# Down-projection with tokens stationary: a decoder layer's MLP on one Trainium2 core

## What is computed

```python
D_MODEL = 2048; D_FF = 8192; LN_EPS = 1e-5; ALPHA = 2 ** 0.25
def layer_norm(x, g, b):
    mu = mean(x); var = mean(square(x - mu))        # over the features
    return (x - mu) * rsqrt(var + LN_EPS) * g + b
# the second half of merge_and_mlp, for every one of the 544 tokens
x1 = layer_norm(ALPHA * x + mixed @ w_out, ln1_g, ln1_b)
u  = maximum(x1 @ w_up, 0)                          # 2048 -> 8192
y  = layer_norm(ALPHA * x1 + (u * u) @ w_down, ln2_g, ln2_b)   # 8192 -> 2048
```

## Time and profile before

| what | value |
|---|---|
| median of three runs | 2963.66 us |
| span of the profiled execution | 2953.3 us |
| PE, DVE, ACT, POOL busy | 95, 64, 29, 7% |
| DVE adds of the down-projection (L2129), 128x544 | 512 of 722 ns |
| DVE remainders of weights (L2116), 128x1024 | 1220 ns |
| ACT roundings of weights (L2041), 128x1024 | 1059 ns |
| a load of w_up or w_down (512 KB), issue to landing | 4.4 us |
| DVE shift of the norm (L2332), when POOL is idle | 0.17 us |

### The profile page before, as it was taken

The page is one execution under the profiler, slowest core; times in us unless marked ns, Lnnn a source line. Parts: engine busy times, 40 slices in busy tenths (PEclk is TensorE's granted clock), DMA queues, the critical chain, the costliest instruction groups (busy, mean ns, idle before and its releaser), DMA issues. The chain is left out here.

```text
span 2953.3 us, 58897 instructions
## 1 busy us (share of the span) xinstructions
PE 2803.1 (95%) x25775; PEld 2658.4 (90%) x25775; DVE 1887.3 (64%) x2204; ACT 842.9 (29%) x1226; POOL 207.3 (7%) x226
## 2 busy tenths in 40 slices
PE   7999999999999887899899999999999999999995
PEld 7998889888887665899789999999999999999994
DVE  3264555455553685536877777777777777777775
ACT  2221222122212355213533233232232322322321
POOL 2011101110110321001000000000000000000003
PEclk9999999999999899999999999999999999999997
DMA  9489999999999722445122232332323323323222
GB/s 343 154 314 402 410 374 412 411 400 394 413 396 340 246 79 82 104 132 138 51 79 86 86 114 71 103 106 67 115 84 88 109 72 107 101 71 115 79 94 89
DMA packets 340851, 548.62 MB, mean 186 GB/s; under 512 B 20940, under 2 KB 244781, under 8 KB 330019
## 3 DMA queue, kind: packets, MB, share of 16 engines
q1 hardware_dynamic: 263682, 334.37, 34.0%
q0 software_dynamic: 13872, 141.28, 11.8%
q10 hardware_dynamic: 63040, 69.21, 6.9%
HBM read 508.96 MB, written 35.84 MB: 184 GB/s over the span
## 5 line engine op out<-in xcount | busy, mean ns | idle before, releaser
L2129 DVE SCALAR_TENSOR_TENSOR base<-big_G,base 128x544 f32<-128x544 f32 x512 | 369.6, 722 | 244.3 <-PE big_G L1964 244.3
L449 PE MATMUL prj_G<-prj_xh,prj_wh 128*128 128x280 f32 x1696 | 504.0, 297 | 20.8 <-DVE prj_wl L692 13.9
L451 PE MATMUL prj_G<-prj_xh,prj_wl 128*128 128x280 f32 x1696 | 498.5, 294 | 0.0
L450 PE MATMUL prj_G<-prj_xl,prj_wh 128*128 128x280 f32 x1696 | 497.8, 294 | 0.0
L699 DVE STREAM_TRANSPOSE prj_kT<-base 128x4096 f32<-128x4096 f32 x64 | 284.5, 4445 | 258.3 <-PE prj_S L482 258.3
L2041 ACT ACTIVATE wh<-raw 128x1024 fp32r<-128x1024 f32 x227 | 239.4, 1059 | 652.8 <-PE big_G L1964 542.8
L1962 PE MATMUL big_G<-ff_uh,wh 128*128 128x272 f32 x1360 | 392.3, 288 | 3.6 <-DVE base L2129 3.5
L1963 PE MATMUL big_G<-ff_ul,wh 128*128 128x272 f32 x1360 | 393.5, 289 | 0.0
L1964 PE MATMUL big_G<-ff_uh,wl 128*128 128x272 f32 x1360 | 393.4, 289 | 0.0
L449 PEld LDWEIGHTS prj_G<-prj_xh,prj_wh 128*128 128x128 f32 x1696 | 322.9, 190 | 46.3 <-issue 34.5
L2116 DVE TENSOR_TENSOR wl<-raw,wh 128x1024 fp32r<-128x1024 f32 x227 | 277.0, 1220 | 86.3 <-ACT wh L2041 86.3
(11 more groups left out here) (418 smaller groups left out, 6097.2 us busy)
## 6 DMA issues: line engine op xcount, KB each, us to landing
prj_v_nat<-in_cache_v SPq DMA_DIRECT2D x242, 512.0 KB, 7.6
raw<-in_w_down SPq DMA_DIRECT2D x128, 512.0 KB, 4.4
raw<-in_w_up SPq DMA_DIRECT2D x120, 512.0 KB, 4.4
prj_raw<-in_w_in ACTq DMA_DIRECT2D x103, 512.0 KB, 17.6
raw<-in_w_out SPq DMA_DIRECT2D x16, 1024.0 KB, 7.1
prj_scratch<-prj_stage ACTq DMA_DIRECT2D x53, 280.0 KB, 9.3
out_xr<-x_scratch SPq DMA_DIRECT2D x16, 544.0 KB, 4.0
base<-in_cache_v SPq DMA_DIRECT2D x14, 512.0 KB, 7.2
```

The costliest lines, as they stand in the source:

```text
L449: mm(out, w_hi[:, k, m], xh[:, k0 + k, cols], start=(first and k == 0), stop=False)
L450: mm(out, w_hi[:, k, m], xl[:, k0 + k, cols], start=False, stop=False)
L451: last = mm(out, w_lo[:, k, m], xh[:, k0 + k, cols], start=False, stop=(end and k == nk - 1))
L2129: V.scalar_tensor_tensor(out, G[2 + t % 2][:, :, 0:HALF_M], 1.0 / ALPHA, out, ALU.mult, ALU.add).then_inc(y_done, 1)
```

## The change

The closing sums are held the other way round, with tokens on partitions: `acc` is 4 tiles of 128 prompt tokens by 2048 features. The first block turns x1 into it: 64 transposes on PE (`turn_back`, 16 ahead of each of the four stages of `up_plain`), copied out by ACT. A half of 272 columns now holds 256 prompt tokens and 16 samples, so that the first layer norm writes each feature tile with two ACT instructions in place of one, into room named `parts`; the combinations of x1 are made in another order and kept there.

**Down-projection.** 128 tokens of uh or ul are stationary and 512 columns of a weight chunk move (`wide`): 96 matmuls a block. A unit is now a pair of token tiles for one chunk, with two banks: G[2] and G[1] alternately (`PAIR`). DVE adds 8 units a block, each 128 x 2 x 512. Since G[1] belongs to the up-projection, `down` waits for all six sums of it (`added`), and the third product of `up` waits for the last add.

**Samples.** The 32 samples are not in the wide matmuls. ACT copies their squared values to `us` (two copies of 128 x 32 ahead of uh), and `sample` multiplies them, in full precision and with the raw weights, in 8 matmuls of 512 columns behind the first chunk of each `down`; the four chunks go to four strips of 32 partitions of one bank, which adds up over all 32 blocks. The loads of the next raw weights wait for it. `sum_samples` turns these sums round in the last block, 24 full-precision matmuls.

**The last block.** It runs token tile by token tile. It has a fourth slot for the weights' halves; the closing norm of a tile follows its adds in the order 0, 1, samples, 2, 3, out of `acc` and in place; `phase_end` is gone. Gain and offset are loaded ahead of it.

```diff
             for k in range(KT):
                 ac.wait_ge(x_done, RS + 2 * k + 2 if k < KT - NSUB else RS + KT - NSUB + k + 1)
-                A(y[:, k, :], y[:, k, :], ACT.Identity, scale=vecs[:, 0, k:k + 1], bias=vecs[:, 1, k:k + 1]).then_inc(x1_done, 1)
+                x1 = part_pair(parts, k)
+                for out, x in ((prompt_columns(x1), two(y[:, k, 0:SEQ])), (sample_columns(x1), two(y[:, k, SEQ:TM]))):
+                    last = A(out, x, ACT.Identity, scale=vecs[:, 0, k:k + 1], bias=vecs[:, 1, k:k + 1])
+                last.then_inc(x1_done, 1)
                 ac.wait_ge(x1_done, k + 1)
-                A(both(xh, k), two(y[:, k, :]), ACT.Copy).then_inc(hh_done, 1)
...
+    NT, WIDE = 4, 512
+    UNITS = 2 * DOWN
+    LAST_BLK = NBLK - 1
...
+        acc = base[:, 0:NT * D].rearrange("p (t n) -> p t n", t=NT)
...
+        us = base[:, few:few + FB * NS].rearrange("p (k n) -> p k n", k=FB)
...
+        PAIR = [G[2], G[1]]
+        SINGLE = [G[2][:, 0, :], G[2][:, 1, :], G[3][:, 0, :]]
+        SAMPLE = G[3][:, 1, :]
...
+        def units_to(b, d):
+            return first_unit(b) + (4 if b == 0 else 2) * (d + 1)
...
+        def unit_out(b, v):
+            if b == LAST_BLK:
+                t, half = divmod(v, 2)
+                return acc[:, t, 2 * WIDE * half:2 * WIDE * (half + 1)].rearrange("p (a n) -> p a n", a=2)
+            d, pair = divmod(v, 2)
+            return acc[:, 2 * pair:2 * pair + 2, WIDE * d:WIDE * (d + 1)]
...
             def ff_block(b, base):
                 for d in range(DOWN):
                     sp.wait_ge(lo_done, base - DOWN + d + 1)
+                    sp.wait_ge(sample_ps, b)
                     load_up(BY_FREE[d], b + 1)
                 for d, n in enumerate((4, 5, 6, 6)):
                     sp.wait_ge(lo_done, base + n + 1)
...
+            def turn_back(kp):
+                if kp > 0:
+                    pe.wait_ge(back_done, NT * kp)
+                for t in range(NT):
+                    for n in range(4):
+                        x = part(2 * (n // 2) + t // 2, kp)[:, n % 2, P * (t % 2):P * (t % 2 + 1)]
+                        last = tr(TURNED[t][:, n * P:(n + 1) * P], x, ident[:, :])
+                    last.then_inc(back_ps, 1)
...
                     if n == 0:
                         pe.wait_ge(added, 6 * b)
+                    elif n == 2:
+                        pe.wait_ge(y_done, first_unit(b))
...
-            def down(b, base, phase, first=False):
+            def wide(out, t, w_hi, w_lo):
+                at = tokens(t)
+                for k in range(FB):
+                    mm(out, uh[:, k, at], w_hi[:, k, :], start=(k == 0), stop=False)
+                    mm(out, ul[:, k, at], w_hi[:, k, :], start=False, stop=False)
+                    last = mm(out, uh[:, k, at], w_lo[:, k, :], start=False, stop=(k == FB - 1))
+                return last
+            def sample(b):
+                for d in range(DOWN):
+                    pe.wait_ge(raw_full[BY_FREE[d]], 16 * down_fill(b))
+                for k in range(FB):
+                    for d in range(DOWN):
+                        last = mm(SAMPLE[NS * d:NS * (d + 1), :], us[:, k, :], down_raw(d)[:, k, :],
+                                  start=(b == 0 and k == 0), stop=(b == LAST_BLK and k == FB - 1))
+                last.then_inc(sample_ps, 1)
...
+            def down_first():
+                pe.wait_ge(low_done, 1)
+                pe.wait_ge(back_done, 4 * NT)
+                for d in range(DOWN):
+                    pe.wait_ge(lo_done, DOWN + d + 1)
+                    w_hi, w_lo = halves_of((ring_h[(DOWN + d) % RING], ring_l[(DOWN + d) % RING]))
+                    for t in range(NT):
+                        v = NT * d + t
+                        if v >= 3:
+                            pe.wait_ge(y_done, v - 2)
+                        wide(SINGLE[v % 3], t, w_hi, w_lo).then_inc(down_ps, 1)
+                    if d == 0:
+                        sample(0)
...
+            def down(b, base):
+                pe.wait_ge(low_done, NLOW + b)
+                pe.wait_ge(added, 6 * b + 6)
                 for d in range(DOWN):
                     pe.wait_ge(lo_done, base + d + 1)
+                    w_hi, w_lo = halves_of((ring_h[(base + d) % RING], ring_l[(base + d) % RING]))
+                    for pair in range(2):
+                        v = 2 * d + pair
+                        pe.wait_ge(y_done, first_unit(b) + (v - 1 if b > 1 or v > 0 else 0))
+                        for t in (2 * pair, 2 * pair + 1):
+                            last = wide(PAIR[v % 2][:, t % 2, :], t, w_hi, w_lo)
+                        last.then_inc(down_ps, 1)
...
-                        pe.wait_ge(low_done, 1 if first else NLOW + b)
-                    slot = (phase + d) % RING
-                    w_hi, w_lo = (flat(x[slot]).rearrange("p (k n) -> p k n", k=FB) for x in (ring_h, ring_l))
-                    for i in range(4):
-                        t = 4 * d + i
-                        if not (first and t < 2):
-                            pe.wait_ge(y_done, KT * b + t - 1)
-                        for c, cols in enumerate(HALVES):
-                            for k in range(FB):
-                                last = third(G[2 + t % 2][:, c, 0:HALF_M], w_hi[:, k, i * P:(i + 1) * P], w_lo[:, k, i * P:(i + 1) * P],
-                                             uh[:, k, cols], ul[:, k, cols], k == 0, k == FB - 1)
+                        sample(b)
+            def down_last(base):
+                pe.wait_ge(low_done, NLOW + LAST_BLK)
+                sample(LAST_BLK)
+                slots = [(ring_h[(base + d) % RING], ring_l[(base + d) % RING]) for d in range(RING)] + [(fourth_h, fourth_l)]
+                for t in range(NT):
+                    for half in range(2):
+                        v = 2 * t + half
+                        pe.wait_ge(y_done, first_unit(LAST_BLK) + v - 1)
+                        for d in (2 * half, 2 * half + 1):
+                            pe.wait_ge(lo_done, base + d + 1)
+                            w_hi, w_lo = halves_of(slots[d])
+                            last = wide(PAIR[v % 2][:, d % 2, :], t, w_hi, w_lo)
                         last.then_inc(down_ps, 1)
+                    if t == 1:
+                        sum_samples()
+            def sum_samples():
+                pe.wait_ge(rows_done, 1)
+                for d in range(DOWN):
+                    mm(ROWS[d], ident[:, NS * d:NS * (d + 1)], rows, start=True, stop=False)
+                    for k in range(4):
+                        last = mm(ROWS[d][:, k * P:(k + 1) * P], x1s[:, 4 * d + k, :], ident[:, :], start=False, stop=(k == 3))
+                last.then_inc(rows_ps, 1)
...
+            for b in range(1, LAST_BLK):
+                base = FIRST + NCH * (b - 1)
+                up(b, base, base)
+                down(b, base + UP)
+            down_last(FIRST + NCH * (NBLK - 2))
...
+                for k in range(FB):
+                    A(two(us[:, k, :]), sample_columns(two(u2[:, k, :])), ACT.Copy)
                 A(uh[:, :, :], u2, ACT.Copy).then_inc(uh_done, 1)
...
+            def take_back(kp):
+                for t in range(NT):
+                    ac.wait_ge(back_ps, NT * kp + t + 1)
+                    out = two(acc[:, t, :])[:, :, 2 * P * kp:2 * P * (kp + 1)]
+                    A(out, two(TURNED[t]), ACT.Copy).then_inc(back_done, 1)
...
+            ac.wait_ge(sample_ps, NBLK)
+            A(rows, SAMPLE, ACT.Copy, scale=1.0 / ALPHA).then_inc(rows_done, 1)
...
+            def add(b, v):
+                dv.wait_ge(down_ps, first_unit(b) + v + 1)
+                out = unit_out(b, v)
+                V.scalar_tensor_tensor(out, PAIR[v % 2][:, :, :], 1.0 / ALPHA, out, ALU.mult, ALU.add).then_inc(y_done, 1)
...
                 add(b, 0)
-                low(base + 9, phase + 9, 1)
+                low(base + 9, 1)
                 add(b, 1)
-                add(b, 2)
                 dv.wait_ge(added, 6 * b + 6)
                 relu_square(b + 1)
+                add(b, 2)
+                low(base + 10, 3)
                 add(b, 3)
...
+            add(b - 1, 7)
             u_low(b)
-            low(base + 2, base + 2, 1)
...
+            low(base + 2, 1)
+            low_to(fourth_l, base + 3, fourth_h, 3)
+            step = Chain(dv, dve)
+            def finish(i):
+                t = CLOSING[i]
+                o = out_s if t == "samples" else acc[:, t, :]
+                dv.wait_ge(small_in, 32)
+                dv.wait_ge(sd_norm, NORM_AT[i])
+                V.tensor_tensor(o, o, gain[0:(NS if t == "samples" else P), :], ALU.mult).then_inc(moments_scale_gain, 1)
+            for i, t in enumerate(CLOSING):
+                r, s = (NS if t == "samples" else P), i % 2
+                if t == "samples":
+                    dv.wait_ge(rows_ps, 1)
+                    for d in range(DOWN):
```

(94 more changed lines are left out.)

459 lines of the change are left out of this document (225 added, 234 removed).

## The result

The changed kernel takes 2987.36 us in the median of four runs (2978.71 to 2993.71), the kernel before 2961.56 beside it: a ratio of 1.0089, with a 95% interval of 1.0063 to 1.0116. It is 26 us slower where 18 less were forecast, and lies above the range.

A forecast was written before the change was run, and what follows sets the result against it. It took TensorE, busy 95% of the 2953.3 us span, as the bound. Loop -7.5, first block and norm +1.5 and the end -12 made -18 us, giving 2945 us, range 2924 to 2980.

The forecast's parts named there:

- The pitch of a matmul: Down-projection: 512-column matmuls start 216 ns apart, between 213.3 and 225.8; 96 take 20.74 us, not 24.16, saving 3.4 a block.
- Rival A: Wide matmuls: the 12.5 ns surcharge stays, so 512 columns take 226 ns; +31 us, 2976 in all; chance 0.17.
- The samples' product: New full-precision matmuls in each down-projection, four strips side by side: 1.97 us a block, range 1.7 to 6.9.
- Rival B: Samples' product: strips don't stream 512 columns side by side; two at a time 3.5 us, 2994; fully serial 3103; chance 0.07.
- The wait at the end of the up-projection: Before each down-projection PE must wait for all six DVE sums and pay for resuming: 0.8 us a block.
- The chain behind uh: Two small ACT copies ahead of uh delay the weight chain to PE's fifth product: 0.4 us a block.
- Covered: DVE's 8 wider sums, about 1.2 us each, and the later loads of up-projection weights stay hidden behind PE's work.
- The loop, summed again: Forecast sum for a loop block: 45.28 us against 45.53, so -0.25 a block and -7.5 us over 30.
- First block and norm: First block with the norm before it: +1.5 us together, between -3 and +5.
- The end: Last down-projection and closing norm, 76.8 us before, run tile by tile with DVE the bound: -12 us, between -20 and -5.

The follow-up runs named there:

- the experiment on the pitch: Changed kernel with the wide matmuls of 20 loop blocks replaced by other lengths, operands or precision, one kind per block; 512 rounded columns took 231.2 ns start to start.

## Why the prediction was wrong

**The pitch of a matmul: the step that failed.** The text took 216 ns for 512 columns, between a bound of 213.3 and one of 225.8. It is 232.7 in the loop, outside both. Thus 96 matmuls take 22.34 us, not 20.74: 1.60 a block, 48 us in the loop's 30. Two errors stand behind it. The upper bound was no bound: it carried the 12.5 ns over as a constant, though one length alone (272 columns) had been seen, from which a constant can't be told from a share; carried over in proportion it would have been 12.5 x 512 / 272 = 23.5, or 236.8, and the truth lies between. A constant comes out nearly right (226.7) only where one and the same stationary operand stays, and in this kernel it changes with every matmul. And 216 came from the row of the nearest length in the earlier trace rows, which is of full precision: the experiment on the pitch shows that full precision has 2.5 ns a record at both lengths, rounded operands 12.5 to 19. The row nearest in kind, 272 rounded columns, was in the loop itself. With 232.7 in its place the loop is 45.28 + 1.60 = 46.88, the sum is 48 higher, 30 over the kernel before, and the sign turns. Rival A had the direction, but not the size (+31 for 226, which alone would still have ended 13 over the kernel before). The Trainium skill, page "TensorE: Matmul & The Clock Gate", section "Wait — 56ns, not 53.3ns?", has N / 2.4 GHz + 2.5 ns: 215.8 here, which the trace contradicts for rounded operands at every length measured (125.9 at 272 columns, where it gives 115.8).

**The samples' product: right.** 1.85 us from its start to the next wide matmul, and 0.09 and 0.11 for the longer distances on either side: 2.05 for 1.97. Without it the loop is 2.08 shorter. Rival B is refuted.

**The wait at the end of the up-projection: right at its place, and its price.** 0.73 idle (2061.07 less 2060.21 and one pitch of 0.13) and 0.08 in the first matmul are the 0.8 forecast. Not in the sum: late loads reach PE through it, 0.12 a block. That nobody else stands behind the wait was right; that others stand ahead of it, a DMA among them, was not said.

**The chain behind uh: right in kind, too high.** 0.4 was taken; the distance ahead of the fifth product grew from 0.22 to 0.40, and moving the copies gives 0.12 back. The two copies take 0.33 together and delay uh by 0.24, where the bounds were 0.4 to 0.55. So the bounds from a 128x1 and a 128x272 activation were both too dear for two in a row.

**Covered: right.** DVE's eight wide additions are 1224 ns each, and no wait for them shows in the loop. The loads of w_up, which now wait for the samples' product, held up neither ACT nor PE; the late ones above are of w_down.

**The loop, summed again** with what was measured: up 21.45, idle 0.73, down 24.46 (22.34 + 0.08 + 2.05) = 46.64, and 0.12 for the late loads. Against the forecast 45.28: +1.60 for the pitch, -0.3 for the chain and the up-projection, +0.1 for the rest, and 0.12.

**First block and norm:** +0.3 in place of +1.5. PE waits 3.51 us for DVE in the new order too, as forecast; the 0.7 forecast for the third ACT instruction does not show, since that stage got 0.7 shorter. Of the three waits before (3.48, 0.88 and 2.85 us) this one is left.

**The end: -12.0, as forecast,** and by the steps named: PE resumes 3.93 us after the loop, DVE is the bound, PE waits 2.39 us for it ahead of its seventh pair, and DVE's small instruction waits for POOL again, as in the earlier trace rows. From DVE's timeline in the changed kernel:

```profile
2957.18 1.41 DVE L2548 SCALAR_TENSOR_TENSOR base<-base 32x1 f32<-32x1 f32 x1
```

While POOL works it takes 1.41, and 0.16 for the token tile before, when POOL is idle; 1.4 was the forecast. That the sum came out to the microsecond is in part luck. DVE's first addition starts at +11.3, not +13; the last gain ends at +51.6, where the text has +52 though its own terms add up to 53; and the first of the last two POOL passes starts beside that gain and stands still, so that POOL ends at +60.4 (forecast +61).

## What to carry to other kernels

A surcharge seen at one length is either a constant or a share, and until a second length is seen the range must hold both (here 226 to 237 ns a matmul); look for the row of the same kind (precision, operands) before the row of the same length. A wait for the last result of a stage costs its idle and also hands on every late transfer ahead of it, so put it at the first instruction that needs it: here one unit later was worth 1.08% of the time, where the whole change had cost 0.89%. What a rearranged product saves has to be set against the remainder that no longer fits it: here 1.8 us of wide matmuls against 2.05 for 32 tokens out of 544.

## What the runs showed of the hardware

At a granted clock of 1.00, matmuls of rounded (fp32r) operands whose stationary operand changes each time follow one another at 4 + 0.447 n ns from 256 to 512 columns, within 1.7 ns; that is 8 to 9% over the bare columns at 512. They are not less than 111.6 ns apart at 192 and 128 columns. With one and the same stationary operand it is 226.7 ns at 512 columns and 125.8 at 272. At full precision, 512 columns take 858 ns, within 1% of four bare passes, and 2.5 ns over them for each of two records, as at 272. Four strips of 32 partitions stream side by side: 8 full-precision matmuls of 512 columns take 1.85 us, where 16 records one after another at 429.2 ns would be 6.9, with 0.1 us on entering that mode and 0.1 on leaving it.
